# The expert stage of a two-block fp32 model on one core: TensorE's straight code for 16 experts against a hardware loop over expert pairs

## The reference, cut to what matters

```python
def expert_choice_ffn(xn, w_router, w_gate, w_up, w_down):
    b, T, d = xn.shape                      # 1, 528, 1024
    cap = CAPACITY_FACTOR * T // N_EXPERTS  # 66
    aff = jax.nn.softmax(jnp.einsum('btd,de->bte', xn, w_router).astype(jnp.float32), axis=-1)
    top_aff, top_idx = lax.top_k(jnp.swapaxes(aff, 1, 2), cap)
    xg = xn[bi, top_idx]
    hg = jnp.einsum('becd,edf->becf', xg, w_gate)
    hu = jnp.einsum('becd,edf->becf', xg, w_up)
    y = jnp.einsum('becf,efd->becd', jax.nn.silu(hg) * hu, w_down)
    y = y * top_aff[..., None].astype(y.dtype)
    return jnp.zeros_like(xn).at[bi, top_idx].add(y)
```

## Time and profile before

| what | value |
|---|---|
| median of 3 runs | 2940.78 us (2939.78 to 2941.17) |
| the profiled execution | 2941.17 us |
| its span, first to last instruction | 2939.4 us |
| TensorE busy | 2694.2 us, 92% |
| VectorE, ScalarE, GpSimd busy | 36%, 22%, 7% |
| HBM read and written | 541.97 MB and 16.29 MB |
| expert stage, per expert | 64.90 us |

### The profile page before, as it was taken

How to read it: one execution, slowest core, us unless ns; L and a number is a source line. 1 busy time by engine, 2 the same in 40 slices (tenths; PEclk the granted TensorE clock), 3 DMA queues, 4 the chain that set the end, 5 groups by cost and what they waited for, 6 DMA issues and landing times.

```text
span 2939.4 us, 39869 instructions
## 1 busy us (share of the span) xinstructions
PE 2694.2 (92%) x17319; PEld 1630.2 (55%) x17319; DVE 1053.2 (36%) x1465; ACT 649.2 (22%) x1153; POOL 209.2 (7%) x218
## 2 busy tenths in 40 slices
PE   5988789999977989989897999699999999999996
PEld 3754437888856777767775998233333333333332
DVE  3236734332215676766684532311111111111111
ACT  3235313222221322314134522200000000000001
POOL 0002000000000201212030000000000000000000
PEclk8998798999989999999999999799999999999998
DMA  3210012222121404123232224799999999999993
GB/s 133 89 55 1 1 57 86 86 99 86 63 103 53 135 31 129 53 69 92 63 102 105 87 87 173 283 389 399 408 397 390 395 396 400 405 398 396 394 394 150
DMA packets 92297, 560.77 MB, mean 191 GB/s; under 512 B 15172, under 2 KB 47940, under 8 KB 59492
## 3 DMA queue, kind: packets, MB, share of 16 engines
q1 hardware_dynamic: 40032, 514.89, 44.4%
q10 hardware_dynamic: 47204, 30.42, 3.9%
q0 software_dynamic: 4896, 12.98, 1.7%
HBM read 541.97 MB, written 16.29 MB: 190 GB/s over the span
## 4 chain that ended last, share of the span: by engine, by line
PE 84%; DVE 7%; ACT 4%; DMA 2%; issue 2%; POOL 0%; ACTq 0%; POOLq 0%; DVEq 0%
PE PS L991 34%; PE PS L487 17%; PE PS L897 4%; PE PS L682 4%; PE PS L678 4%; PE PS L679 4%; PE PS L902 2%; PE PS L651 2%; PE PS L500 2%; PE PS L547 1%; PE PS L543 1%; PE PS L544 1%; PE PS L583 1%; DMA H<-h_t 1%; PE PS L981 1%
## 5 line engine op out<-in xcount | busy, mean ns | idle before, releaser
L487 PE MATMUL PS<-U,ring 128*128 128x264 f32 (+1 forms) x2336 | 556.6, 399 | 28.6 <-DVE arena L1704 18.7
L487 PEld LDWEIGHTS PS<-U,ring 128*128 128x128 f32 (+1 forms) x2336 | 455.5, 197 | 123.4 <-issue 32.4
L991 PE MATMUL PS<-expert_ring_low,U 128*32 128x512 f32 x4608 | 510.5, 595 | 0.9 <-DVE U L1918 0.9
L991 PE MATMUL PS<-expert_ring_high,U 128*32 128x512 f32 x4608 | 504.8, 592 | 0.0
L991 PEld LDWEIGHTS PS<-expert_ring_high,U 128*32 128x32 f32 x4608 | 148.0, 110 | 336.9 <-issue 335.9
L991 PEld LDWEIGHTS PS<-expert_ring_low,U 128*32 128x32 f32 x4608 | 146.3, 110 | 333.4 <-issue 332.4
L1693 DVE SCALAR_TENSOR_TENSOR H<-arena,par,H 128x528 f32<-128x528 f32 x240 | 189.3, 834 | 1.4
L1930 DVE TENSOR_TENSOR H<-H,PS 128x512 f32<-128x512 f32 x32 | 22.0, 688 | 440.5 <-PE PS L991 425.0
L678 PE MATMUL PS<-UX,WF 128*128 128x512 f32 x352 | 140.0, 398 | 11.7 <-DVE UX L1500 11.6
L679 PE MATMUL PS<-UX,WF 128*128 128x512 f32 x352 | 138.8, 394 | 0.0
L1438 ACT ACTIVATE H<-PS 128x512 f32<-128x512 f32 x32 | 19.1, 597 | 475.6 <-PE PS L991 475.6
(11 more groups left out here) (317 smaller groups left out, 3233.8 us busy)
## 6 DMA issues: line engine op xcount, KB each, us to landing
expert_ring_low<-w_experts SPq DMA_DIRECT2D x96, 2048.0 KB, 11.2
expert_ring_high<-w_experts SPq DMA_DIRECT2D x96, 2048.0 KB, 11.2
ring<-w_gu SPq DMA_DIRECT2D x11, 2048.0 KB, 7.8
ring<-ssd_sums ACTq DMA_DIRECT2D x32, 512.0 KB, 7.9
ring<-w_in SPq DMA_DIRECT2D x6, 2048.0 KB, 8.0
ring<-w_xbc SPq DMA_DIRECT2D x8, 1536.0 KB, 6.5
ring<-w_down SPq DMA_DIRECT2D x8, 1408.0 KB, 5.9
ring<-w_conf SPq DMA_DIRECT2D x8, 1024.0 KB, 5.4
```

Source lines behind the costliest of these rows:

```text
L487: last = nc.tensor.matmul(PS[0:M, banks[i], 0:hi - lo], lhs(k), rhs(k)[:, lo:hi], start=(k == 0), stop=(k == K - 1))
L991: mm = nc.tensor.matmul(PS[QUAD * t:QUAD * t + QUAD, bank, :], stat(t), move(t), start=start, stop=stop)
```

## The change

TensorE's sixteen written-out experts become: the first pair in straight code, pairs 1 to 6 as a hardware loop whose body is two experts, and the last pair in straight code. The functions that are called are the same; inside the loop `pair` is a register, so the semaphore values of the waits are computed from it while the program runs. Semaphores, buffers and the programs of the other engines stay as they are.

```diff
             turn_x(0)
-            for e in range(EXPERTS):
-                expert(e // 2, e % 2, turn_next=e < EXPERTS - 1)
+            expert(0, 0)
+            expert(0, 1)
+            with pe.Fori(1, EXPERTS // 2 - 1) as pair:
+                expert(pair, 0)
+                expert(pair, 1)
+            expert(EXPERTS // 2 - 1, 0)
+            expert(EXPERTS // 2 - 1, 1, turn_next=False)
```

## The result

The changed kernel takes 2973.05 us (median of 4, 2971.38 to 2977.62) against 2940.98 us for the kernel before in the same series: the ratio is 1.0112, with a 95% interval of 1.0096 to 1.0128. It is slower by 32 us. The forecast was 2955 us, the range 2941 to 2972 us: the sign was right, the forecast rise of 14 us was less than half of the measured one, and the time lies 1 us above the range. The profiled execution took 2975.13 us, with a span of 2973.4 us, 34 us more than that of before.

A forecast was written before the change was run, and what follows sets the result against it. The prediction took TensorE to bound the expert stage, with no gap to fill. Five jumps at 1.6 us of exposed fetch plus 1.2 us of clock gave 14 us, 2955 us for the median; the range was 2941 to 2972 us.

The forecast's parts named there:

- What bounds the kernel: Expert stage: bound by TensorE without idle gaps, so unhidden additions to its stream lengthen the end one for one.
- the 26 us of ready weights: Expert stage: weights lie ready some 26 us early, so a TensorE pause of 2 to 5 us fits.
- (1): Loop edges: five jumps back, at experts 4, 6, 8, 10 and 12; at least 0.2 us each, 1 us in all.
- (5): Loop body: 22 register waits per expert, costed at nothing; 21 us in all if their cover were gone.
- (6): Other engines in the expert stage: they shift with TensorE and release nothing late; nothing is given back.
- (2): Each jump back: fetching the packet at the loop's start takes 3.7 us, bounds 0 and 9.2 us.
- (3): Each jump back: work already handed over covers 2.1 us of the fetch, leaving a 1.6 us gap, 8 us for five.
- (4): After each jump's gap: half clock loses 1.5 us in 7 of 9 cases, so 1.2 us per edge.
- A: Jumps back: sequencer lead hides the fetch, each edge costs 0 to 0.3 us, 2941 to 2943 us; chance 0.25.
- B: Loop body: stays held, nothing refetched, q8 moves 47 packets fewer, 0.2 us per edge, 2942 us; chance 0.05.
- C: Jumps back: fetch waits like data, 9.2 us, an edge costs 8.6 us, 43 us in all, 2984 us; chance 0.07.
- D: Looped experts: register waits thin out TensorE's stream without a visible gap, up to 21 us, 2962 us; chance 0.05.

The follow-up runs named there:

- single-round loops: Changed kernel with pairs 1 to 6 in six loops of one round each, register waits kept, no jump back taken: 2941.18 us, ratio 1.0003.
- with 512: Changed kernel, each load of expert weights after the first eight moving 512 of 4096 columns, stale weights multiplied: 2951.87 us, one run.
- with 2048 columns: Changed kernel, each load of expert weights after the first eight moving 2048 of 4096 columns, stale weights multiplied: 2962.31 us, one run.

## Why the prediction was half right

What bounds the kernel was right: every microsecond added to TensorE's stream came out at the end, and the 26 us of ready weights covered the pauses.

(1) Five jumps, their places, and none on entering or leaving: right; that q8 would stay at about 137 packets was not. (5) Register waits at nothing: right, shown by the single-round loops. (6) Nothing late elsewhere: right, experts between jumps take 64.90 us.

(2) The price of the fetch is the term that failed. I took 3.7 us, from a 256 KB load where the queues are calm plus the 1.1 us of an instruction packet. A fetch with nothing ahead of it costs 3.9 to 4.4 us even in the quiet stage, near to that; under load it is 4.7 to 6.6 us, measured at the second packet. The step from calm to loaded was sized from how long a packet occupies its engine, and that is alike in both (1.01 us on average with all columns, 1.05 with 512); what grew was the time until it begins to move. The one argument that q8 isn't held up as the weights are rests on a slip: 96.1% of 16 x 900 us / 24113 is 0.57 us for a weight packet, not 5.7, so an instruction packet occupies its engine longer than a weight packet, not far shorter.

(3) The cover, chosen as a middle at 2.1 us, measured 1.2 to 3.2 us, so whether it was mis-sized stays open. Together the two terms gave a gap of 1.6 us where 4.0 was measured, 12 us over five jumps.

(4) The clock: 6 us forecast, 6.0 us measured, and that is luck. It fell at three of five jumps, not at 7 of 9, but cost 2.0 us each time and not 1.5. The nine gaps were not all: of the 27 gaps of 1.5 us and more between 920 and 1635 us of the kernel before, 16 were followed by half clock.

Missing altogether was the second packet: 7.5 us in the changed kernel, 3.1 of them as gaps, and 17.9 us of gaps in the kernel with its head at place 236. I had counted the packets of the body and not asked at which place in one the loop begins.

Of the rivals, A named the right contest, lead against fetch, and lost since the fetch is longer than the lead. B is refuted by 150 packets. C, with 9.2 us, has the right cause, traffic of weights, and too high a price; the argument against it was the slip above. D is refuted.

## What to carry to other kernels

A hardware loop had no gap where its body was held (1024 instructions here); a body of 1792 or 2400 was fetched again each round. Then each jump back costs the fetch less what the engine has queued, and in a stage full of DMA traffic this came, with the clock and the packet's border, to 6 to 7 us, too little to notice once and 32 us after five. Count instructions, not lines, before you loop an engine that sets the end. If the loop must stay, announce the jump and begin the body at the start of a packet, both together: the one alone gave back 13 of 32 us, the other nothing.

## What was not expected of the hardware

In straight running only the next packet of instructions is on its way (no two overlap in the kernel before, 1940 to 2840 us). It is asked for when the one before it is entered (4.7 to 6.6 us from entry to use under load), so a loop head near the end of a packet pays twice. At a jump two can be on their way: with 2048 columns the target's packet moved from 2271.94 to 2273.41 us and another, by the order the unneeded one behind the body's end, from 2271.87 to 2274.22. And a gap of 3.4 to 4.5 us was followed by half clock at 5 of 5 jumps in one kernel and at 3 of 5 in another, where the two without it had a second gap instead.
